# A two-block sequence model on one core: another order of the first mixers, seven block products for the mixers' output, and other places in the second product

## The reference, cut to what matters

```python
def first_block(x, p, ...):
    hn = rms_norm(h, norm_mix_g)
    z_a, z_b, z_c, z_d = _split(hn @ w_in, [A_COLS, B_COLS, C_COLS, D_COLS])
    o_a = gmlp_spatial_gating(z_a, ...)      # "gm": gu, gv
    o_b = gated_deltanet(z_b, ...)           # "dn": q, k, v, dg and a chunked solve
    o_c = rwkv7_time_mix(z_c, ...)           # "rw": r, rk, rv, rx and a chunked solve
    o_d = conformer_conv(z_d, ...)           # "cf": cz, cs, 31 taps, layer norm
    h = h + concatenate([o_a, o_b, o_c, o_d]) @ w_out
    hn = rms_norm(h, norm_ffn_g)
    gate = causal_depthwise_conv(hn @ w_ffn_gate, ffn_conv_w)
    h = h + (silu(gate) * (hn @ w_ffn_up)) @ w_ffn_down
    hn = rms_norm(h, norm_ple_g)
    h = h + (p @ w_ple_proj) * sigmoid(hn @ w_ple_gate)
    return rms_norm(h, final_norm_g)

def second_block(x, mem, ...):
    y = concatenate([ssd_mixer(...), s5_mixer(...), rglru_mixer(...)]) @ w_out
    h = layer_norm(ALPHA * h + y)
    h = layer_norm(ALPHA * h + cross_attention(h, mem, ...))
    return layer_norm(ALPHA * h + square(relu(h @ w1)) @ w2)
```

## Time and profile before

| | |
|---|---|
| three runs | 3241.03, 3246.91, 3248.35 us; median 3246.91 |
| the profiled execution: its own time | 3250.28 us |
| its span (first to last instruction) | 3248.4 us |
| mean granted TensorE clock | 0.986 of full speed |
| PE busy | 3134.3 us, 96% |
| DVE, POOL, ACT busy | 1816.2, 1121.9, 775.6 us |

### The profile page before, as it was taken

How to read it: one execution, slowest core, us unless ns; L and a number is a source line. 1 busy time by engine, 2 the same in 40 slices (tenths; PEclk the granted TensorE clock), 3 DMA queues, 4 the chain that set the end, 5 groups by cost and what they waited for, 6 DMA issues and landing times.

```text
span 3248.4 us, 32378 instructions
## 1 busy us (share of the span) xinstructions
PE 3134.3 (96%) x12306; PEld 1923.9 (59%) x12306; DVE 1816.2 (56%) x2558; ACT 775.6 (24%) x1304; POOL 1121.9 (35%) x855
## 2 busy tenths in 40 slices
PE   8989998999999999998999999999999999999997
PEld 3446463874444444587744454544554588888886
DVE  2387876742444344476733745654124655577876
ACT  3333334321111111000122343403212344410002
POOL 0010030003334333455611000153014698865555
PEclk9999999999999999999999999999999999999998
DMA  4211102142222122465312212202112233366652
GB/s 139 65 52 40 41 29 65 53 169 65 78 91 91 62 97 84 156 239 198 139 58 74 65 52 65 66 26 91 65 39 91 104 136 141 120 223 250 226 192 88
DMA packets 206121, 334.88 MB, mean 103 GB/s; under 512 B 10128, under 2 KB 123280, under 8 KB 205200
## 3 DMA queue, kind: packets, MB, share of 16 engines
q1 hardware_dynamic: 205968, 332.81, 29.6%
HBM read 268.55 MB, written 64.23 MB: 102 GB/s over the span
## 4 chain that ended last, share of the span: by engine, by line
PE 83%; DVE 10%; POOL 3%; ACT 2%; issue 1%; DMA 1%; DVEq 0%; SPq 0%; POOLq 0%; ACTq 0%
PE psum L1891 16%; PE psum L3698 15%; PE psum L181 10%; PE psum L3452 7%; PE psum L402 7%; PE psum L2511 7%; PE psum L1936 3%; PE psum L4259 3%; DVE arena L1337 2%; DVE arena L1335 2%; PE psum L3469 1%; PE psum L555 1%; PE psum L4236 1%; PE psum L4197 1%; PE psum L1942 1%
## 5 line engine op out<-in xcount | busy, mean ns | idle before, releaser
L3698 PE MATMUL psum<-arena 128*128 128x256 f32 x2660 | 582.5, 382 | 14.5 <-DVE arena L3744 7.0
L3698 PEld LDWEIGHTS psum<-arena 128*128 128x128 f32 x2660 | 508.7, 192 | 87.4 <-issue 9.2
L1891 PE MATMUL psum<-arena 128*128 128x512 f32 x1232 | 530.1, 592 | 1.9 <-DVE arena L2269 1.9
L1891 PEld LDWEIGHTS psum<-arena 128*128 128x128 f32 x1232 | 233.7, 190 | 296.6 <-issue 291.5
L402 PE MATMUL psum<-arena 128*128 128x512 f32 x768 | 337.1, 598 | 4.9 <-DVE arena L1193 4.9
L181 PE MATMUL psum<-arena 128*128 128x512 f32 x768 | 332.4, 592 | 1.5 <-ACT arena L4429 1.5
L2191 DVE TENSOR_TENSOR arena<-arena,psum 128x512 f32<-128x512 f32 x176 | 116.9, 685 | 295.3 <-PE psum L1891 154.8
L402 PEld LDWEIGHTS psum<-arena 128*128 128x128 f32 x768 | 146.5, 192 | 188.8 <-issue 187.0
L3452 PE MATMUL psum<-arena 128*128 128x256 f32 x1080 | 246.0, 381 | 10.1 <-ACT small_sb L3489 4.0
L181 PEld LDWEIGHTS psum<-arena 128*128 128x128 f32 x768 | 145.8, 190 | 182.1 <-issue 180.6
L2511 PE MATMUL psum<-arena 128*128 128x512 f32 x576 | 250.9, 594 | 0.0
(11 more groups left out here) (546 smaller groups left out, 4418.1 us busy)
## 6 DMA issues: line engine op xcount, KB each, us to landing
arena<-w_in SPq DMA_DIRECT2D x42, 1024.0 KB, 5.3
arena<-mlp_w SPq DMA_DIRECT2D x72, 512.0 KB, 7.1
arena<-w_ffn_down SPq DMA_DIRECT2D x36, 512.0 KB, 6.8
arena<-mlp_w SPq DMA_DIRECT2D x8, 2048.0 KB, 8.7
mlp_hidden_T<-arena SPq DMA_DIRECT2D x32, 512.0 KB, 2.6
arena<-mlp_hidden_T SPq DMA_DIRECT2D x16, 1024.0 KB, 5.6
arena<-w_out SPq DMA_DIRECT2D x12, 1024.0 KB, 5.2
mlp_hidden_B<-arena SPq DMA_DIRECT2D x24, 512.0 KB, 2.7
```

The lines of the kernel that those rows point to most:

```text
L1891: mm = nc.tensor.matmul(ps, left, right, start=(k == 0), stop=(k == 3))
L3698: mm = self.env.nc.tensor.matmul(ps[:, 256 * r:256 * r + 256], left[:, s, r * P:(r + 1) * P], right[:, s, :], start=(first and s == 0 and ...
```

## The change

Five parts of the program are changed. (1) The first mixers run in another order on PE, ACT and DVE: unit `cs(1)` moves from behind `v(1)` to before `chunks("dn", 0)`; `query_norm` is cut from `dn_values` and stands a unit later; unit `gu(1)` moves before `dn_rates(1)`; the layer norms `gm` (h = 1) and `rw` (h = 0) are interleaved, and unit `r(1)` is cut in halves around `dn_grams(1)`, unit `rx(1)` around `key_norm(1)`. The conformer's taps stand at other places. (2) `w_out` becomes a product of blocks like gate and up, 4 times 7 products of 4 matmuls each; POOL makes 20 sums of weight blocks and 12 of inputs, DVE 8 of inputs. (3) In the second product the second raw block of m1 = 7 gets two slots of its own, and each wide addition stands behind the `right_sums` of an item of its own. (4) `sum_squares(3)` stands one output tile later. (5) Two of the squared-ReLU layer's four kinds of activation (R11, R22) stand behind that item's copies.

Cut to its core (`...` where lines are left out):

```diff
 # PE, first mixers
             dn_values(0)
+            query_norm(0)
             unit("rk", 0, 1800)
...
             layer("gm", 0)
+            unit("cs", 1, 2824)
             chunks("dn", 0)
             dots(0)
             unit("k", 1, 768)
             dn_norm(0)
             rows_ab(1)
+            mix_tokens(0)
             unit("v", 1, 1024)
-            mix_tokens(0)
-            unit("cs", 1, 2824)
             spread_tokens(0)
             rw_tokens(0)
...
             unit("dg", 1, 1280)
+            query_norm(1)
+            unit("gu", 1, 0)
             dn_rates(1)
-            unit("gu", 1, 0)
             unit("gv", 1, 256)
             chunks("rw", 0)
-            layer("gm", 1)
             rw_centre(0)
-            dn_grams(1, lambda: rw_variance(0))
-            unit("r", 1, 1544)
+            layer_centre("gm", 1)
+            rw_variance(0)
+            layer_variance("gm", 1)
+            gates = unit_steps("r", 1, 1544)
+            next(gates)
+            dn_grams(1)
+            next(gates)
...
             unit("rv", 1, 2056)
+            low_rank = unit_steps("rx", 1, 2312)
+            next(low_rank)
             key_norm(1)
-            unit("rx", 1, 2312)
+            next(low_rank)
 # ACT, first mixers
             mixes("rk", 1, 1)
-            key_squares(1)
-            layer("cf", 0)
+            layer("cf", 0, lambda: key_squares(1))
 # DVE, first mixers
             bonus(0)
-            some(taps, 16)
             conv("k", 1)
...
             taps = taps_of(1)
-            some(taps, 42)
+            some(taps, 20)
             solve("rw", 0)
             carry("rw", 0)
-            some(taps, 62)
+            some(taps, 24)
             layer("gm", 1)
             rw_final(0)
+            mix("r", 0, 1, (0,))
             dn_grams(1)
             steps = inverse("dn", 1)
...
             spread_out(1)
+            some(taps, 9)
             mix("rv", 2, 1)
+            some(taps, 62)
             mix("rx", 3, 1)
             layer("cf", 1)
 # PE, output of the mixers
-            finish(mix[0].steps(pe, lambda k: half_of(env, O0, k, 0)))
-            for i in mix[1].steps(pe, lambda k: half_of(env, O0, k, 1), mixed):
-                if i == 0:
+            for n in range(4):
+                mixed(2, n)
+                mixed(4, n)
+            for n in range(4):
+                for m in (5, 1, 7):
+                    mixed(m, n)
+            for n in range(4):
+                mixed(3, n)
+                mixed(6, n)
+                if n == 0:
                     sum_squares(0)
 # POOL, output of the mixers: ahead of add_sq(0, range(8)); what follows is as before
+            for k in range(4):
+                p_sum.mark(g_.tensor_tensor(mix_new["D21"][k], mix_a(1, k, 0), mix_a(0, k, 0), ALU.subtract), "m", "D21", k)
+            pool.wait_ge(mixers["mem_out"], 32)
+            for n in range(3):
+                mix_sums(2, n)
+            pool.wait_ge(mixers["rw_out"], 4)
+            for k in range(4):
+                p_sum.mark(g_.tensor_tensor(mix_new["N1"][k], mix_a(0, k, 0), mix_a(1, k, 1), ALU.add), "m", "N1", k)
...
+                p_sum.mark(g_.tensor_tensor(mix_a(1, k, 0), mix_a(1, k, 0), mix_a(1, k, 1), ALU.add), "m", "N3", k)
+            mix_sums(2, 3)
+            for n in range(4):
+                for m in (5, 1, 7):
+                    mix_sums(m, n)
+            for n in range(4):
+                mix_sums(6, n)
             add_sq(0, range(8))
             add_sq(1, range(3))
             weights(0)
             add_sq(1, range(3, 4))
             differences_of_x()
             add_sq(1, range(4, 5))
             weights(1)
             add_sq(1, range(5, 8))
 # DVE, output of the mixers
-            for i in range(8):
-                add(mix[0], i, 0)
-            add(mix[1], 0, 1)
-            scale(0)
-            for i in range(1, 8):
-                add(mix[1], i, 1)
...
+            for n in range(4):
+                mixed(3, n)
+                if n == 1:
+                    scale(0)
+                mixed(6, n)
 # second product
-    late_added = {1: (), 5: (), 6: ("U2", "R00"), 7: ("U3", "U4", "C22", "R01", "R11"), 4: ("C21", "R10"), 2: (), 3: ()}
+    late_added = {11: "U2", 13: "R00", 15: "U3", 16: "U4", 17: "C22", 18: "R01", 19: "R11", 20: "C21", 21: "R10"}
...
-                if g == 3:
-                    for name in late_added[m1]:
-                        add_late(name)
+                if n in late_added:
+                    add_late(late_added[n])
 # second product, SP's loads
+        if n in self.of_apart:
+            earlier = [was for was, r in self.of_apart.items() if r == self.of_apart[n] - len(self.apart)]
+            if earlier:
+                self.blocks.wait(sp, "late", "S", earlier[0])
+            else:
+                before(sp, n, 1)
+            for c in range(self.parts(n)):
+                sp.dma_start(self.a_slot(n, 1, 0)[:, c], self.view(0, c, g)[:, :, HALF:2 * HALF]
+                             ).then_inc(self.apart[self.of_apart[n] % len(self.apart)][1], 16)
 # small gated layer (PE, ACT and DVE)
-                    if i == 0:
+                    if i == 1 - h:
                         sum_squares(3 + h, after)
 # squared-ReLU layer, ACT
-                    squared_relu(n - 2)
+                    squared_relu([key for key in activated_after(n - 2) if key not in activated_late(n)])
                 if two_level(n - 1):
                     quads.copy(act, n - 1, "c21")
                 if n < LAST_N:
                     quads.copy(act, n, "t2")
+                squared_relu(activated_late(n))
```

More of the change, by code:

```diff
@@ L1126, in _ @@
             layer("gm", 0)
+            glu_sigmoid(1)
             chunks("dn", 0)
@@ L2019, in _ @@
                 if v < 2:
-                    sp.wait_ge(unit_done, 2 * (plan.units - SLOTS + v + 1))
+                    tiles.wait(sp, "mix", v, 6)
                 else:
@@ L2184, in scale, with mixed @@
                     tiles.release(dve, "root", n)
-            def add(product, i, h):
-                product.wait_done(dve, i)
-                product.take(v_.tensor_tensor(y(i, h), y(i, h), product.out(i), ALU.add), i)
             def into(dst, key, op=ALU.add):
                 return v_.tensor_tensor(dst, dst, tiles.ps(*key), op)
+            def mixed(m, n):
+                y11, y12, y21, y22 = [y(2 * n + i, h) for i in range(2) for h in range(2)]
+                parts = {2: ((y21, ALU.add), (y22, ALU.subtract)), 6: ((y22, ALU.add),), 5: ((y11, ALU.subtract), (y12, ALU.add)),
+                         1: ((y11, ALU.add), (y22, ALU.add)), 7: ((y11, ALU.add),), 3: ((y12, ALU.add), (y22, ALU.add)),
+                         4: ((y11, ALU.add), (y21, ALU.add))}
+                before = {4: 2, 5: 4, 1: 5, 7: 1, 3: 1, 6: 3}
+                tiles.wait(dve, "mix", n, m)
+                if m in before:
+                    tiles.wait_taken(dve, "mix", n, before[m])
+                for dst, op in parts[m]:
+                    ins = into(dst, ("mix", n, m), op)
+                tiles.take(ins, "mix", n, m)
             def part_a(kind, g):
```

186 lines of the change are left out of this document (139 added, 47 removed).

## The result

| | before | after |
|---|---|---|
| median, lowest to highest (4 runs each) | 3245.3 us (3241.03 to 3248.35) | 3224.2 us (3223.54 to 3226.61) |
| ratio of the times, 95% interval | | 0.9936 (0.9923 to 0.9948) |
| the profiled execution, and its span | 3250.28, 3248.4 us | 3226.61, 3224.7 us |

A forecast was written before the change was run, and what follows sets the result against it. PE, busy 96% of the span, was taken as the bound. Parts 1 to 3 (-10, -3.9, -9.4), 4 and 5 (-2.1, -3) sum to -28.4: 3250.28 becomes 3221.9 us, or 3219 for a timed run; range 3203 to 3238.

The forecast's parts named there:

- some 7 us: First mixers, second half: how much sooner DVE gets its grams (4.9, and the wait, less 6.9 of half r(1)).
- the 4.56 us: First mixers, second half: a PE wait that half of r(1) was to cover, with its slow clock.
- the better bound: Part 1, first mixers: bound of -14 us, with no slow clock and mixes free; -10 was taken.
- 6 to 10: Sign for part 2: a PE wait of 6 to 10 us at the sum of squares behind the output product.
- weights 6.16: Output product, POOL's list: five weight sums take 6.16 us, from 82.6 to 88.8 after PE's first matmul.
- `scale(0)`, 3.35 + 5.39 us: Output product: DVE work between products (3,1) and (6,1), so that the fourth square comes at 91 us.
- `scale(0)` is over before the sums that count: Output product: reason why eight new DVE sums and `scale(0)` would not slow POOL, leaving its sums at 1.23 us.
- +14: Part 2's slow bound: POOL's 26 us from 82.6 on stretch to 44 beside DVE's sums; -4 was taken.
- 2.13 us a sum: Price behind part 2's slow bound: four POOL additions took 8.51 us beside DVE's wide sums, instead of 1.26 each.
- The 7.04 and 4.53 us: Second product: two PE waits that part 3 was to remove, -15.2 us together with the slow clock.
- the last rival, SP blocked: Second product: new slots hold SP's in-order list, hidden values behind wait; part 3 +29, total +10, 3257 us; chance 0.06.
- a wait on a load in the second product: Sign against the forecast: it falls if the second product still shows such a wait.

The follow-up runs named there:

- e1: Changed kernel with sixteen of the 24 taps back ahead of the convolution of k (half 1): 3213.56 us, ratio 0.9894.
- e2: Changed kernel where POOL makes only the weight sums PE's first product needs ahead of the last additions of squares, the other eight behind: 3216.41 us, ratio 0.9901.
- e7: Changed kernel with the wide addition R10 behind item 20 instead of 21 in the second product, one run: 3219.81 us.
- e3: Changed kernel with the fourth residual load issued two items later, ahead of item 23's loads instead of 21's, one run: 3224.18 us.
- e4: Changed kernel without part 5, activations R11 and R22 again ahead of the copies, one run: 3228.33 us.
- e5: Changed kernel with sixteen taps back ahead of the convolution of k; POOL makes one weight sum, all additions of squares, differences, then other weight sums: 3204.15 us, ratio 0.9869.

## Why the prediction was right, and where it was off

**Part 1, -14.1 against -10.** The mechanism came as worked out. The wait for the turned tiles was 17.22 us ("some 17"), its releaser `spread_out` behind the 24 taps; the grams began at 322.90 (323); the layer norm of the conformer at 536.62 (538.5) after 7.64 us (8 to 9), released by a tap. e1 shows the cause of the first wait by taking it away. The "some 7 us" by which DVE gets its grams sooner was 7.8, though the terms printed for it give 2.6 (4.9 + 4.56 - 6.9); the slow clock behind the 4.56 us and two small waits beside it went as well, and `chunks("rw", 0)` began 6.4 us sooner instead of 4.9. The gain at the layer norm is 14.1 us, 1.9 more than worked out; the slow clock cost 1.7 there (5.28 us against 3.60), charged at 1.8. A wait of 2.20 us on DVE at 504.39, ahead of that row, was not foreseen. The stage ended at the better bound for a reason that the prediction doesn't have: a wait of 2.4 us on DVE that both kernels show was followed by the slow clock before (the stretch 672 to 676 has 0.64) and not after (1.00 from 660 on), which gives another 1.6 us. PE's rows, before and after:

```profile
672.79 5.47 PE L535 MATMUL psum<-arena 128*128 128x128 f32 x32 [2.45 <-DVE arena L1348]
```

```profile
660.32 3.84 PE L543 MATMUL psum<-arena 128*128 128x128 f32 x32 [2.38 <-DVE arena L1391]
```

All nine experiments have 3.84 us there as well, behind waits of 2.4 to 2.5. Why is open, so these 1.6 us are luck.

**Part 2, +2.6 against -3.9: the term that was mis-sized.** The mechanism is the one predicted, POOL's list ahead of the last additions, and the releaser is POOL, as stated. But the wait was 12.47 us, not 7.8 and outside the 6 to 10 that the prediction gave as its sign, and the slow clock behind it cost 3.7 us, not 1.8. The gain became a loss. The step that failed is "weights 6.16" beside "`scale(0)`, 3.35 + 5.39 us": both rows come from a kernel in which neither ran beside the other. Now they overlap, `scale(0)` takes 4.05 us more, product (6,1)'s addition with it, and the fourth square came at 95.4 us from the start, not 91. From there on the sum of the prediction, 17.5 us to POOL's end, holds to 0.1 us (95.4 to 113.0). e2 shows it from the other side: without the sums beside it `scale(0)` is 5.39 us; the stretch is 9.6 shorter, which is that and the shorter list together. The price stood in the trace of the kernel before, some 60 us behind the place that the prediction read, where DVE's sums of x meet POOL's. DVE's row and POOL's, before:

```profile
837.87 1.64 DVE L2269 TENSOR_TENSOR arena<-arena 128x512 f32<-128x512 f32 x1
```

```profile
837.25 1.71 POOL L2343 TENSOR_TENSOR arena<-arena 128x512 f32<-128x512 f32 x1
```

The prediction had weighed the rule of the Trainium skill that speaks of this (GPSIMD Engine Reference, section 8, Key points) and set it aside because "`scale(0)` is over before the sums that count"; it is over before them, but it delays what they wait for. The rule was right here, in direction (9.44 us against 5.39), and the +14 that the prediction gave as its far end was too much. Its 2.13 us a sum is a mean of unlike cases: one addition took 3.31 us beside a wide sum of DVE, the other three 1.59 to 1.77 beside sums of 128x512.

**Part 3, -11.6 against -9.4.** The 7.04 and 4.53 us are gone, and at item 23 stands a wait of 4.16 us ("3 to 5"), of which e7 takes 1.5 away by R10's place. The 2.2 us beyond the forecast have no term in it: before, PE also waited 2.39 us for POOL at 1598.60, which nobody named and which is gone after; what removed it was not tried. Not foreseen either was the 1.68 us wait one item earlier, which e3 ties to the load of the residual in SP's list. This was the mechanism of the last rival, SP blocked, and a wait on a load in the second product, which the prediction had named as a sign against itself; it came in a form too small to show in the time, since e3 gains 0.5 us at most. SP's own timeline shows it between two rows:

```profile
1492.88 0.99 SPq L3800 DMA_DIRECT2D arena<-w_ffn_down  x2
1515.73 0.37 SPq L2093 DMA_DIRECT2D arena<-ffn_residual  x1
```

For 22 us nothing is issued, until the residual load at 1515.73 may go (DVE's addition R01 that it waits for ended at 1515.71), and the weights behind it come late.

**Parts 4 and 5.** Part 4 gave 2.3 us (2.1). Part 5 is worth some 2 us by e4, where 3 were forecast. Against the kernel before it gained nothing all the same: at its two places stand 3.30 us on POOL (2573.37) in place of the 2.95 on ACT, and 2.75 on DVE (2845.88) in place of 1.02 and 1.50. The prediction allowed for that with its upper end of 0. Beyond it 1.6 us were lost between 2024.60 and the program's end, 0.6 of them ahead of these places. Some 0.7 more of them lie in the squared-ReLU layer's last product and what follows it, which takes 375.4 to 377.8 us in the ten kernels after the change (before: 377.1), and so are within the spread. Why POOL and DVE are later at the two places was not tried.

Summed up: 4.1 us better in part 1 and 2.2 in part 3, 6.5 worse in part 2 and 4.6 behind part 4 make, with 0.2 better in part 4, the 4.7 us by which the predicted gain of 28.4 was too large for this span. That the time came within 6 us of the forecast is luck in part: errors of 2 to 7 us in both directions cancelled for the most part, and part 2 had the wrong sign.

## What to carry to other kernels

A duration read where an operation ran alone must be worked out anew where the change puts it beside another engine's work on the same memory: here eight scalings went from 5.39 to 9.44 us, which with the longer slow clock behind the wait turned a forecast gain of 3.9 into a loss of 2.6. Work moved out of an engine's idle time costs its whole length at the next place where another engine waits for that engine, so first see whether the old place was free (16 taps, 10.8 us). In a list that runs in order, put ahead of a wanted result only what the waiting engine needs next; here that was worth 15 us to the output stage, 5 of which came back as contention further on.

## What the runs showed of the hardware

One DVE sum of 128x512 took 9.90 us, where the next took 0.69. POOL was in a run of 17 sums without a pause, and DVE's sum ended (734.66) as that run did (734.11); POOL kept its 1.23 us a sum. All eight experiments that keep part 2 show the same (9.90 to 9.92 us, ending 0.55 us behind POOL's run). Rows of DVE, then of POOL, after the change:

```profile
724.76 9.90 DVE L2348 TENSOR_TENSOR arena<-arena 128x512 f32<-128x512 f32 x1
734.69 0.69 DVE L2350 TENSOR_TENSOR arena<-arena 128x512 f32<-128x512 f32 x1
```

```profile
713.25 20.86 POOL L285 TENSOR_TENSOR arena<-arena 128x512 f32<-128x512 f32 x17
```

The eight scalings of `scale(0)` show the other face of this meeting. Taken one by one, the four that began at 781.17, 782.84, 784.52 and 786.20 took 1.75 us each and the others 0.74 to 0.75; the four are those beside which POOL's weight sums ran on, at 1.71 to 1.80 us each. That is what the sums show in e5 (1.64 to 1.75 us on DVE, 1.71 on POOL). So the same meeting has two faces in these runs: DVE held up until POOL is through (9.90 us), or both slowed by turns. DVE's operations with an input in PSUM kept their times beside POOL (0.67 to 0.69 us). What chooses between the two is not settled by these runs.

The price of the slow clock behind a wait differed too: 3.7 us of extra length behind the 12.47 us, against 1.8 behind the 9.74 of the earlier trace rows; granted clock 0.50 in both.
